# A decoder layer on one core: three of eight token tiles take their experts from streamed blocks in place of gathered rows

## The chip, the cores and the metric

The kernel runs on one core of a Trainium2 chip. The metric is the device time of one execution in microseconds (us), the median of three runs. All arithmetic is fp32. TensorE (PE) multiplies, VectorE (DVE) and ScalarE (ACT) do elementwise work, GpSimd (POOL) issues the gathers, SyncE (SP) issues the direct DMAs. Each engine works off its own instructions in order and waits on semaphores.

## The reference

One layer over 1024 tokens of width 1024: a mixer (attention and pooling, gated and merged), a norm, and then PEER, a mixture of 16384 single-neuron experts, of which each token uses 16 in each of 8 heads, and a last norm:

```python
s = einsum('chpk,hpnk->chpn', q, sub_keys)            # 2 x 128 scores for each head
s1, i1 = top_k(s[:, :, 0], 16);  s2, i2 = top_k(s[:, :, 1], 16)
cand = s1[..., :, None] + s2[..., None, :]            # 256 sums, the best 16 of them
sc, ci = top_k(cand, 16)
idx = row * 128 + col                                 # expert = row * 128 + column
gate = softmax(sc)
act = gelu(einsum('ched,cd->che', u[idx], y))
out = einsum('che,ched->cd', gate * act, v[idx])      # v rows weighted and summed
h = layer_norm(ALPHA * h + out)
```

## The kernel before

Tokens are in 8 tiles of 128 (P). The mixer works on them in three groups of 2, 3 and 3 tiles (`GTS`). All its steps have due times, called ticks here: `unit_at` (products with `w_in`), `step_at` (one step of attention: one head, one tile), `branch_at`, `norm_at`, `query_at`. Each engine has generators that yield such times; `merged` puts them in the order of their times, and `woven` gives a function `advance(tick)` that issues everything that is due by then.

The experts are worked off in slots. A slot t = 128 n + 16 h + e is one gathered row of experts: expert e of head h for each of the 128 tokens of tile n. There are 1024 slots. For each one GpSimd gathers 128 lines of 8 KB (`u` and `v` of an expert side by side, array `uv`) into a ring of 8 (L759). VectorE multiplies the `u` half with the tokens and sums it to one number per token (L1361, `product`). ScalarE takes Gelu for two slots (L950) and multiplies by the gate (L954). Then the `v` half is summed in one of two ways: for even slots, and for all slots from slot 726 on, ScalarE makes a diagonal matrix of the coefficients (L963) and TensorE multiplies it with the row (L1648, `spread`, in two halves, sums kept in PSUM); for 292 odd slots (`by_vector`) VectorE multiplies and adds to `z` (L1313, `add_row`). `join` (L1298, L1300) puts the two sums together, and `norm_step` does the last norm, spread over the slots of the next tile. VectorE also finds the experts, 24 slots ahead, in small steps between the rows: `retrieve`, L1211 to L1276, 64 heads of 18 steps.

The mixer and the slots run together: before slot 0 every engine does the ticks below 0 (group 0), and after each slot t it calls `advance(t)`. So a tick is a slot, and group 1 is due at ticks 0 to about 312, group 2 up to about 726 (its queries and search scores at ticks 598 to 726). Scores of most tiles go to DRAM (`s_scr`) and come back when they are searched; tiles 3 and 4 are parked in `y_scr`.

The lines the change touches in VectorE's loop:

```python
for slot in range(SLOTS):
    product(n, slot)
    if t >= 2 and by_vector(t - 2):
        add_row(t - 2)
    ...                                   # two, one or no steps of the search
    advance(SLOTS * n + slot)
```

Of the kernel before, what the change touches and what calls it, by code (L numbers as in the profile page):

```python
# [8 lines left out]
F32 = mybir.dt.float32  # L9
# [6 lines left out]
P = 128  # L16
# [10 lines left out]
RH = 8  # L27
# [14 lines left out]
DIAGS = 4  # L42
NEG = -3.0e38
PE_AHEAD = 2
# [8 lines left out]
LAST_SLOT = SLOTS * TT  # L53
# [10 lines left out]
DIRECT = T0S[:-1]  # L64
LOADED = [n for n in range(SAVED) if n not in DIRECT]

GATES_AT = (1,) * (H - 1) + (9,)
SEQ = [("p", i) for i in range(NP)] + [(r, 0) for r in "qkv"]
for _h in range(H):
# [10 lines left out]
               tuple(range(598, 598 + 16 * RH + 1, 16)))  # L80
# [10 lines left out]
PARKED = (T0S[1] + 1, T0S[1] + 2)  # L91
# [128 lines left out]
def by_vector(t):  # L220
    if not (24 if t >= SLOTS else 3) <= t % SLOTS < SLOTS - 4:
        return False
    return t % 2 == 1 and t < score_at(NG - 1, RH)

PE_SUMS = list(itertools.accumulate(0 if by_vector(t) else 1 for t in range(LAST_SLOT)))
DVE_SUMS = list(itertools.accumulate(1 if by_vector(t) else 0 for t in range(LAST_SLOT)))

BASED = [n for n in range(TT) if any(by_vector(t) for t in range(SLOTS * n, SLOTS * (n + 1)))]  # L230

# [17 lines left out]
def lent(slot):  # L250

    return slot >= 78 and 14 <= slot % SLOTS < 118

def values_lent(g, k):
    return g > 0 and lent(step_at(g, k) + DO_VALUES[g])

def output_lent(g, k):
    return g > 0 and lent(step_at(g, k) + DO_OT[g])  # L260

def scores_behind(g, k):

    at = step_at(g, k) + DO_OT[g]
    return sum(2 for j in range(NSTEPS[g]) for c in range(len(chunks(g, j))) if score_chunk_at(g, j, c) <= at) + score_no(
        g, 0, 0, 0)

def output_behind(g, k):  # L270

    at = [j for j in range(NSTEPS[g]) if not output_lent(g, j) and step_at(g, j) + DO_OT[g] < step_at(g, k)]
    return STEP0[g] + at[-1] + 1 if g and at else 0

def last_lent(n, is_lent, offset):

    uses = [STEP0[g] + k for g in range(1, NG) for k in range(NSTEPS[g])
            if is_lent(g, k) and (step_at(g, k) + offset[g]) // SLOTS == n]
    return uses[-1] + 1 if uses else 0  # L280

def exponent_at(g):

    begin = TOPK * g - SEARCH_AHEAD + 14
    steps = [step_at(j, k) + DO_EXP[j] for j in range(1, NG) for k in range(NSTEPS[j])]
    return min([slot for slot in steps if begin <= slot < begin + 6], default=begin)

def build(nc, ctx, a, ident, k_scr, v_scr, b_scr, y_scr, s_scr, out):  # L290
# [68 lines left out]
    diag = [at(f"diag{i}", 176 + 0.5 * i, [P, P]) for i in range(DIAGS)]  # L359
# [6 lines left out]
    z = at("z_e", 189, [P, D])  # L366
    yn = at("yn_e", 193, [P, D])
# [63 lines left out]
    def sem(name):  # L431
        return ctx.enter_context(nc.semaphore("r_" + name))
# [1272 lines left out]
```

## Time and profile before

| | |
|---|---|
| median of 3 runs | 3284.1 us (3283.27 to 3287.0) |
| span of the profiled execution | 3285.6 us |
| bytes moved | 1245 MB |
| TensorE, VectorE, ScalarE, GpSimd busy | 2791, 2433, 1145, 1353 us |
| gathers | 1024, of 1.05 MB |

### The profile page before, as it was taken

How to read it: one execution, taken by the hardware profiler on the slowest of the kernel's cores; microseconds unless marked ns; L12 is line 12 of the kernel's file. 1: busy time of each engine (PE TensorE's matmuls, PEld its weight loads, DVE VectorE, ACT ScalarE, POOL GpSimd, SP SyncE). 2: the span in 40 equal slices, each digit the busy share in tenths (PEclk: the TensorE clock that was granted, in tenths of full speed). 3: DMA queues.
4: the chain of work that ended last, by engine and by line, in shares of the span. 5: the costliest groups of instructions: out<-in, count | busy, mean ns of one | idle time of the engine just before them, and what ended most of it. 6: DMA issues, size and time to landing. Idle time of an engine off the chain costs nothing.

```text
span 3285.6 us, 30165 instructions
## 1 busy us (share of the span) xinstructions
PE 2791.3 (85%) x8360; PEld 1440.5 (44%) x8360; DVE 2432.9 (74%) x5863; ACT 1144.9 (35%) x3457; POOL 1353.1 (41%) x1248
## 2 busy tenths in 40 slices
PE   9999999999986899888989898867866777777776
PEld 7776555555433445444444444323433222222222
DVE  2216778995888778997799878798788676667664
ACT  2302455553223333444445322222323333333332
POOL 1101345654434444453455543344445444444442
PEclk9999999999998999999999999989999999999999
DMA  5635999999999999998999999999999999999997
GB/s 195 246 134 200 368 386 371 405 411 369 419 392 411 421 420 404 420 398 332 351 394 385 382 420 420 396 382 421 420 417 420 422 415 417 415 418 416 420 414 311
DMA packets 205223, 1244.97 MB, mean 379 GB/s; under 512 B 23680, under 2 KB 36992, under 8 KB 73600
## 3 DMA queue, kind: packets, MB, share of 16 engines
q0 software_dynamic: 147456, 1073.81, 80.4%
q1 hardware_dynamic: 56592, 169.11, 13.7%
q8 instruction: 67, 1.10, 0.1%
q14 instruction: 100, 0.82, 0.1%
q10 hardware_dynamic: 1008, 0.14, 0.0%
HBM read 1228.81 MB, written 14.16 MB: 378 GB/s over the span
## 4 chain that ended last, share of the span: by engine, by line
PE 44%; DMA 30%; DVE 15%; issue 5%; ACT 4%; POOL 1%; SPq 0%; POOLq 0%; DVEq 0%; ACTq 0%
DMA ring<-uv,idx 29%; PE r_o L1648 16%; PE w_ps L1428 15%; DVE ring L1361 7%; DVE z_e L1313 3%; PE r_o L1614 1%; PE w_ps L1476 1%; PE w_ps L1580 1%; PE w_ps L1557 1%; POOL ring L759 1%; PE w_ps L1614 1%; ACT diag L963 1%; PE r_o L1521 1%; PE r_o L1557 1%; PE r_o L1580 1%
## 5 line engine op out<-in xcount | busy, mean ns | idle before, releaser
L759 POOL DMA_INDIRECT ring<-uv,idx x1024 | 1193.5, 1166 | 1655.6 <-PE r_o L1648 1230.7
L1648 PE MATMUL r_o<-ring,diag 128*128 128x512 f32 x2928 | 1454.8, 631 | 436.6 <-ACT diag L963 424.3
L1361 DVE CUSTOM_DVE_ANT_0 ring<-ring,ytok 128x1024 f32<-128x1024 f32 x768 | 936.7, 1221 | 233.5 <-DMA ring<-uv,idx 230.7
L1648 PEld LDWEIGHTS r_o<-ring,diag 128*128 128x128 f32 x2928 | 542.3, 197 | 1173.7 <-ACT diag L963 643.0
L1428 PE MATMUL w_ps<-x,w 128*128 128x384 f32 (+1 forms) x2112 | 653.0, 456 | 11.0 <-DMA x<-xT 5.7
L950 ACT ACTIVATE gel<-dot 128x2 f32<-128x2 f32 x512 | 104.1, 203 | 1577.1 <-DVE dot L1361 1576.2
L1428 PEld LDWEIGHTS w_ps<-x,w 128*128 128x128 f32 x2112 | 396.9, 192 | 230.6 <-issue 58.7
L1361 DVE CUSTOM_DVE_ANT_0 ring<-ring,zn 128x1024 f32<-128x1024 f32 x256 | 313.3, 1224 | 210.5 <-DMA ring<-uv,idx 209.5
L1313 DVE SCALAR_TENSOR_TENSOR z_e<-ring,coef,z_e 128x1024 f32<-128x1024 f32 x292 | 375.0, 1284 | 0.0
L963 ACT ACTIVATE diag<-ident,coef 128x128 f32<-128x128 f32 x732 | 262.2, 387 | 0.0
L954 ACT ACTIVATE coef<-gel,gate 128x1 f32<-128x1 f32 x1024 | 245.9, 287 | 16.8
L1614 PE MATMUL w_ps<-yT,wq 128*128 128x384 f32 x512 | 190.3, 492 | 0.0
L1614 PEld LDWEIGHTS w_ps<-yT,wq 128*128 128x128 f32 x512 | 100.8, 197 | 103.3 <-issue 70.9
L950 ACT ACT_TABLE_LOAD x94 | 120.6, 1283 | 1.6
L1090 DVE CUSTOM_DVE_ANT_0 e<-w_ps,bias 128x512 f32<-128x512 f32 (+3 forms) x160 | 93.1, 593 | 33.8 <-PE w_ps L1476 32.2
L835 ACT ACTIVATE e<-e,st_a 128x384 f32<-128x384 f32 (+5 forms) x128 | 98.1, 769 | 1.0 <-DVE st_a L1094 0.5
L724 POOL TENSOR_SCALAR st_a<-st_a 128x1 f32<-128x1 f32 x64 | 28.8, 450 | 159.1 <-ACT junk L871 157.5
L1476 PE MATMUL w_ps<-k,q 64*128 64x512 f32 (+3 forms) x320 | 81.2, 585 | 11.9 <-ACT o L861 8.8
L1557 PE MATMUL w_ps<-o,wc 128*128 128x384 f32 x256 | 90.6, 488 | 0.0
L1361 DVE DVE_READ_ACCUMULATOR2_ANT dot<- 128x1 f32 x1024 | 84.7, 83 | 0.0
L848 ACT ACTIVATE aT<-w_ps 128x512 f32<-128x512 f32 (+2 forms) x96 | 46.2, 481 | 85.6 <-PE w_ps L1495 79.9
L1557 PEld LDWEIGHTS w_ps<-o,wc 128*128 128x128 f32 x256 | 48.8, 191 | 42.6 <-issue 19.4
(198 smaller groups left out, 2331.9 us busy)
## 6 DMA issues: line engine op xcount, KB each, us to landing
w<-w_in SPq DMA_DIRECT2D x132, 512.0 KB, 3.7
wq<-wq SPq DMA_DIRECT2D x46, 512.0 KB
wc<-w_branch SPq DMA_DIRECT2D x24, 768.0 KB, 5.7
ring<-uv,idx POOLq DMA_INDIRECT x1024
wo<-w_out SPq DMA_DIRECT2D x24, 512.0 KB, 11.6
xs<-x SPq DMA_DIRECT2D x8, 512.0 KB, 7.5
out<-yn_e SPq DMA_DIRECT2D x8, 512.0 KB
x<-xT SPq DMA_DIRECT2D x16, 192.0 KB, 5.5
```

The lines of the kernel that those rows point to most:

```text
L759: nc.gpsimd.indirect_dma_start(out=ring[t % RING][:], out_offset=None, in_=a["uv"], in_offset=bass.IndirectOffsetOnAxis(ap=idx[:, slot:slo ...
L835: nc.scalar.activation(e[g][k % 2][:, wh, 0:n], e[g][k % 2][:, wh, 0:n], ACT.Exp, bias=nmx[:, wh:wh + 1], accum_out=den[:, wh:wh + 1]).the ...
L950: nc.scalar.activation(gel[:, slot:slot + GROUP], dot[:, slot:slot + GROUP], ACT.Gelu).then_inc(gelu_out, 1)
L954: nc.scalar.activation(coef[:, slot + j:slot + j + 1], gel[:, slot + j:slot + j + 1], ACT.Copy, scale=gate[:, h, e_:e_ + 1]).then_inc(coef ...
L963: nc.scalar.activation(diag[u % DIAGS][:], ident[:], ACT.Copy, scale=coef[:, slot + j:slot + j + 1]).then_inc(diag_ready, 1)
L1313: nc.vector.scalar_tensor_tensor(z[:], ring[t % RING][:, D:], coef[:, slot:slot + 1], z[:], ALU.mult, ALU.add).then_inc(vsummed, 1)
L1361: nc.vector.tensor_tensor_reduce(ring[r][:, 0:D], ring[r][:, 0:D], y_of(n)[:], 1.0, 0.0, ALU.mult, ALU.add, dot[:, slot:slot + 1]).then_in ...
L1428: ins = nc.tensor.matmul(bank, w_raw[g][i % RAWS][:, c, :], x_raw[g][:, c, :], start=c == 0, stop=c == DC - 1)
L1476: nc.tensor.matmul(score_bank(g, wh)[:, 0:n], q[g][h % 2][rows, qs], keys[g][h % 2][rows, begin:begin + n], start=True, stop=True).then_in ...
L1557: ins = nc.tensor.matmul(bank, branch_weights(g, n)[:, j, :], o_all[g][:, j, :], start=j == 0, stop=j == CA - 1)
L1614: ins = nc.tensor.matmul(query_bank(g)[:, 0:WS[g]], query_weights(g, i)[:, c * P:(c + 1) * P], yT[g][c // 4][:, c % 4, :], start=c == 0, s ...
L1648: ins = nc.tensor.matmul(o_ps[n % 2][half][:], diag[(u - 1) % DIAGS][:], ring[t % RING][:, D + half * HALF:D + (half + 1) * HALF], start=s ...
```

## The change

Slots are kept for the first five tiles alone (`GT = 5`, 640 slots). In them VectorE sums every row: `spread`, the diagonals, `join` and the banks lent between the two uses go. Each of two `z` takes every second tile. The sum of a row stands 3 slots behind its product (`LAG`).

The last three tiles (`DT = 3`, 384 tokens) are multiplied with all 16384 experts, in 128 blocks of 128 experts. Block b loads 512 KB of `uT` (3 buffers), TensorE makes the scores of 384 tokens (8 products of 128x384), ScalarE takes Gelu from PSUM, VectorE multiplies by the gates of the block (128x384, most of them zero), and TensorE multiplies with 512 KB of `v` (6 products of 128x512, sums kept in six PSUM banks over all blocks). The scores are 7 blocks ahead of the sums (`LEAD`).

The gates come as follows: the search for the 24 heads of these tiles is the same as before, but its steps follow each other with few rows between (`dense_found`). Rows, columns and shares are transposed; for each of the 384 tokens VectorE makes two one-hot matrices of 128x128 (`dense_hots`), TensorE multiplies them to the 128x128 gates of this token (`places`), ScalarE copies them out, and they go to DRAM (`g_scr`, 12 chunks of 2 MB) and come back for 8 blocks at a time (`gates_in`, 1 KB pieces).

A tick is not a slot any more. `KNOTS` maps slots to ticks: 0 to 165 on 0 to 616, 165 to 187 on 616 to 880, 187 to 640 on 880 to 2092. VectorE, ScalarE, GpSimd and SyncE call `advance(tick_at(t))`. TensorE has no slots left; it does its merged order and waits on semaphores alone. Queries of group 2 take 11 ticks a head in place of 16 and end at tick 686. The dense sums are due from tick 960, 9 ticks a block.

```diff
+GT = 5
+DT = TT - GT
-LAST_SLOT = SLOTS * TT
+LAST_SLOT = SLOTS * GT
...
-               tuple(range(598, 598 + 16 * RH + 1, 16)))
+               tuple(range(598, 598 + 11 * RH + 1, 11)))
...
+NUB, NVB, NGEL, NOH, GQ = 3, 4, 8, 8, 8
+LEAD = NGEL - 1
+EARLY_S = 5
+FOUND_AT = tuple(SCORE_TIMES[2][0] + 18 + 11 * m for m in range(DT * RH + 1))
+TURN_AT = tuple(FOUND_AT[RH * (i + 1)] + 4 for i in range(DT))
+OH_LEN = 3.5
+T_D = TURN_AT[-1] + 6 + int(OH_LEN * P / NOH) + 14
+BLOCK = 9
+KNOTS = ((0, 0), (165, 616), (187, 880), (LAST_SLOT, T_D + BLOCK * NK - 20))
...
+def sum_at(b):
+    return T_D + BLOCK * b
+def dense_at(b):
+    if b < EARLY_S:
+        return SCORE_TIMES[2][RH] + 4 + 5 * b
+    if b < LEAD:
+        return TURN_AT[1] + 2 + 6 * (b - EARLY_S)
+    return sum_at(b - LEAD) + 5
```

SyncE (loads of blocks, gates out and in):

```diff
+        def up_in():
+            for b in range(NK):
+                yield dense_at(b - NUB) + 5 if b >= NUB else norm_at(2, DT) + 12 + b
...
+                sp.dma_start(ub[b % NUB][:], a["uT"][b]).then_inc(u_in[b % NUB], 16)
+        def down_in():
...
+                sp.dma_start(vb[b % NVB][:], a["v"][b * P:(b + 1) * P]).then_inc(v_in[b % NVB], 16)
+        def gates_out():
+            for c in range(CHUNKS):
+                yield hot_at((c + 1) * CHUNK // NOH - 1) + 8
+                sp.wait_ge(place_copied, (c + 1) * CHUNK // 4)
+                sp.dma_start(g_scr[c], stage_g[c % 2][:]).then_inc(g_out[c % 2], 16)
+        def gates_in():
...
+                sp.dma_start(gq[q % 2][:].rearrange("p c r t -> p c (r t)"),
+                             g_scr[:, :, GQ * q:GQ * (q + 1), :].rearrange("c p r t -> p c (r t)")).then_inc(g_in[q % 2], 16)
```

GpSimd, ScalarE and VectorE:

```diff
                 if t >= RING:
-                    if by_vector(t - RING):
-                        pool.wait_ge(vsummed, DVE_SUMS[t - RING])
-                    else:
-                        pool.wait_ge(summed, PE_SUMS[t - RING])
+                    pool.wait_ge(vsummed, t - RING + 1)
...
-                advance(t - RING)
+                advance(tick_at(t - RING + LAG))
...
+                nc.scalar.activation(gel_d[b % NGEL][:], dense_bank(b)[:, 0:DENSE], ACT.Gelu).then_inc(gel_done, 1)
...
-                nc.scalar.activation(diag[u % DIAGS][:], ident[:], ACT.Copy,
-                                     scale=coef[:, slot + j:slot + j + 1]).then_inc(diag_ready, 1)
...
+                for j in range(NOH):
+                    t = NOH * c + j
+                    nc.vector.tensor_scalar(hot_r[u % 2][:, j], count_d[:], turned_d[:, 0, t:t + 1], turned_d[:, 2, t:t + 1],
+                                            ALU.is_equal, ALU.mult)
+                    ins = nc.vector.tensor_scalar(hot_c[u % 2][:, j], count_d[:], turned_d[:, 1, t:t + 1], None, ALU.is_equal)
...
+        def dense_gates():
+            for b in range(NK):
+                yield sum_at(b) - 9
+                dve.wait_ge(gel_done, b + 1)
...
+                nc.vector.tensor_tensor(tokens, tokens, gq[b // GQ % 2][:, :, b % GQ], ALU.mult).then_inc(a_done, 1)
...
-        for n in range(TT):
+        for n in range(GT):
...
                 product(n, slot)
                 t = SLOTS * n + slot
-                if t >= 2 and by_vector(t - 2):
-                    add_row(t - 2)
+                if t >= LAG:
+                    add_row(t - LAG)
...
-                advance(SLOTS * n + slot)
+                advance(tick_at(t))
```

TensorE:

```diff
+        def dense_scores():
+            for b in range(NK):
+                yield dense_at(b)
+                pe.wait_ge(u_in[b % NUB], 16 * (b // NUB + 1))
+                if b >= 2:
+                    pe.wait_ge(gel_done, b - 1)
+                for c in range(DC):
+                    ins = nc.tensor.matmul(dense_bank(b)[:, 0:DENSE], ub[b % NUB][:, c], yT[2][c // 4][:, c % 4, :],
+                                           start=c == 0, stop=c == DC - 1)
+                ins.then_inc(u_done, 1)
+        def dense_sums():
+            for b in range(NK):
+                yield sum_at(b)
+                pe.wait_ge(v_in[b % NVB], 16 * (b // NVB + 1))
...
+                pe.wait_ge(a_done, b + 1)
+                for i in range(DT):
+                    for half in range(2):
+                        ins = nc.tensor.matmul(sum_bank(i, half)[:], gel_d[b % NGEL][:, i * P:(i + 1) * P],
+                                               vb[b % NVB][:, half * HALF:(half + 1) * HALF], start=b == 0, stop=b == NK - 1)
...
-        advance = woven(all_stages(stage))
-        advance(-1)
-        for n in range(TT):
-            for slot in range(SLOTS):
-                if not by_vector(SLOTS * n + slot):
-                    spread(n, slot)
-                advance(SLOTS * n + slot + PE_AHEAD)
+        for _ in merged(all_stages(stage), rcg_turns(), places(), dense_scores(), dense_sums()):
+            pass
```

Smaller parts: all first norms of groups 1 and 2 have their `x` loaded at once, the search scores of all of tiles 0 to 4 but the first four heads go through `s_scr`, the attention of groups 1 and 2 has the banks `o_ps[0]` for its values and outputs, and some semaphores are shared.

## Rows read from the trace of the kernel before

**Rows 1.** The page: span, busy time of each engine, and DMA share in 40 slices.
```profile
span 3285.6 us, 30165 instructions
PE 2791.3 (85%) x8360; PEld 1440.5 (44%) x8360; DVE 2432.9 (74%) x5863; ACT 1144.9 (35%) x3457; POOL 1353.1 (41%) x1248
...
DMA  5635999999999999998999999999999999999997
```

**Rows 2.** Busy time of every engine by stretch; the first line names the columns.
```profile
core 0: us, PE busy (x) PEld busy (x) DVE busy (x) ACT busy (x) POOL busy (x), PEclk, DMA share, GB/s
0.00:302.80 302.80, 289.12 (x1296) 224.81 (x1297) 83.11 (x285) 64.14 (x211) 32.59 (x71) 1.00 0.50 174
302.80:731.00 428.20, 416.42 (x1516) 241.56 (x1515) 367.26 (x919) 216.15 (x585) 213.71 (x190) 1.00 0.98 389
731.00:1300.00 569.00, 501.86 (x1363) 251.32 (x1362) 443.69 (x997) 172.07 (x543) 228.75 (x202) 0.96 1.00 405
1300.00:1900.00 600.00, 530.57 (x1781) 274.68 (x1779) 518.46 (x1246) 272.69 (x731) 297.67 (x266) 0.95 0.97 382
1900.00:2624.00 724.00, 568.84 (x1378) 259.85 (x1379) 580.78 (x1328) 210.89 (x685) 317.65 (x269) 0.94 1.01 413
2624.00:3110.00 486.00, 360.91 (x768) 140.28 (x767) 337.91 (x870) 158.11 (x530) 202.52 (x194) 0.99 1.01 417
```

**Rows 3.** The same for L1361 alone, two records a slot.
```profile
2624.00:3110.00 486.00, 236.47 (x384) 0.99 1.01 417
```

**Rows 4.** The page: DMA queues, with packets, MB and share of 16 engines.
```profile
q0 software_dynamic: 147456, 1073.81, 80.4%
q1 hardware_dynamic: 56592, 169.11, 13.7%
```

**Rows 5.** The page: groups by line; busy us, mean ns | idle before, releaser.
```profile
L759 POOL DMA_INDIRECT ring<-uv,idx x1024 | 1193.5, 1166 | 1655.6 <-PE r_o L1648 1230.7
L1648 PE MATMUL r_o<-ring,diag 128*128 128x512 f32 x2928 | 1454.8, 631 | 436.6 <-ACT diag L963 424.3
...
L1614 PE MATMUL w_ps<-yT,wq 128*128 128x384 f32 x512 | 190.3, 492 | 0.0
...
L950 ACT ACT_TABLE_LOAD x94 | 120.6, 1283 | 1.6
```

**Rows 6.** TensorE: L1614's records (ns min/median/max), two runs of records (start, length).
```profile
L1614 PE MATMUL w_ps<-yT,wq x512: 486/486/847, 1013.7 to 2516.3; 128*128 128x384 f32 x171
...
234.04 27.70 PE r_o L1580 x64
...
2510.36 1.45 PE L1614 MATMUL w_ps<-yT,wq 128*128 128x384 f32 x4
```

**Rows 7.** VectorE in order of time (start, length): a row, and a head's search alone.
```profile
562.48 1.22 DVE L1361 CUSTOM_DVE_ANT_0 ring<-ring,ytok 128x1024 f32<-128x1024 f32 x1
563.62 0.09 DVE L1361 DVE_READ_ACCUMULATOR2_ANT dot<- 128x1 f32 x1
563.62 1.28 DVE L1313 SCALAR_TENSOR_TENSOR z_e<-ring,coef,z_e 128x1024 f32<-128x1024 f32 x1
564.82 0.48 DVE L1224 MAX8 top<-s 128x8 f32<-128x128 f32 x2
...
286.13 0.49 DVE L1211 MAX8 top<-s 128x8 f32<-128x128 f32 x2 [7.46 <-ACT s L912]
...
295.63 0.17 DVE L1274 SCALAR_TENSOR_TENSOR idx<-rc 128x16 uint32<-128x16 f32 x1
```

**Rows 8.** VectorE, single lines: duration ns min/median/max, first and last start.
```profile
L1101 DVE TENSOR_SCALAR st_a<-st_a x64: 272/272/274, 40.8 to 1851.1; 128x1 f32<-128x1 f32 x64
L1083 DVE TENSOR_SCALAR bias<-bias x24: 680/686/690, 26.6 to 1785.2; 128x1024 f32<-128x1024 f32 x24
L1288 DVE TENSOR_SCALAR gate<-gate,esum x64: 222/229/233, 298.8 to 3227.8; 128x16 f32<-128x16 f32 x64
L1047 DVE TENSOR_TENSOR pad<-pad x30: 427/567/620, 11.9 to 1269.7; 128x399 f32<-128x399 f32 x8, 128x397 f32<-128x397 f32 x6, 128x271 f32<-128x271 f32 x4, 128x393 f32<-128x393 f32 x4
```

**Rows 9.** VectorE's waits from 2600 to 3270 us: total, times, longest.
```profile
DVE ring L1361 <- DMA ring<-uv,idx: 216.0, 212, 2.2
```

**Rows 10.** VectorE in order of time: last product and last operation.
```profile
3268.84 1.23 DVE L1361 CUSTOM_DVE_ANT_0 ring<-ring,zn 128x1024 f32<-128x1024 f32 x1 [1.22 <-DMA ring<-uv,idx]
...
3281.29 1.23 DVE L1339 TENSOR_TENSOR yn_e<-yn_e,gb_e 128x1024 f32<-128x1024 f32 x1
```

More of the change, by code:

```diff
@@ L63 @@
 SAVED = KTS[NG - 2]
-DIRECT = T0S[:-1]
-LOADED = [n for n in range(SAVED) if n not in DIRECT]
+HEADS_KEPT = SBUFS
 GATES_AT = (1,) * (H - 1) + (9,)
@@ L217, in final_pad @@
     return 2 - i % 2
[L220 to L230, printed above, removed]
 class Place:
@@ L247, in score_chunk_at, with build @@
     return step_at(g, k) + SCORE_GAP[g] * c
[L250 to L280, printed above, removed]
 def exponent_at(g):
-    begin = TOPK * g - SEARCH_AHEAD + 14
+    begin = tick_at(TOPK * g - SEARCH_AHEAD + 14)
     steps = [step_at(j, k) + DO_EXP[j] for j in range(1, NG) for k in range(NSTEPS[j])]
-    return min([slot for slot in steps if begin <= slot < begin + 6], default=begin)
-def build(nc, ctx, a, ident, k_scr, v_scr, b_scr, y_scr, s_scr, out):
+    return min([tick for tick in steps if begin <= tick < tick_at(TOPK * g - SEARCH_AHEAD + 20)], default=begin)
+def build(nc, ctx, a, ident, k_scr, v_scr, b_scr, y_scr, s_scr, g_scr, out):
     at = Place(nc)
@@ L474, in build, with weights_of @@
     block = ctx.enter_context(nc.Block())
+    def weights_of(r):
+        return len(range(r, UNITS, RAWS))
     def osb_of(g, k):
@@ L647, in scores_out @@
         def scores_out(g):
-            rows = slice(T0S[g] + 1, KTS[g])
+            rows = slice(T0S[g], KTS[g])
             for h in range(RH):
@@ L933, in shares @@
         def shares():
-            for g in range(1, RH * TT):
+            for g in range(1, RH * GT):
                 yield exponent_at(g)
@@ L979, in _ @@
         advance(-1)
-        for n in range(TT):
+        for n in range(GT):
             for slot in range(0, SLOTS, GROUP):
                 coefficients(n, slot)
-                if n and slot == 20:
+                if n and slot == 18:
                     normalize(n - 1)
-                advance(SLOTS * n + slot + GROUP)
-        normalize(TT - 1)
+                advance(tick_at(SLOTS * n + slot + GROUP))
+        normalize(GT - 1)
+        advance(END)
     @block.vector
@@ L1199, in retrieve @@
+        steps_done, steps_d_done = [0], [0]
         def retrieve(g):
             h = g % RH
[L1203 to L1217 removed]
@@ L1269, in retrieve @@
-            assert done == PER * (g + 1)
-            yield
-            dve.wait_ge(step, done)
+            yield from found(scores_of(g), top, topi, topf, s2, cand, cand2, hot, best[:, h], besti, ab, abf, rc[:, 0],
+                             rc[:, 1], step, steps_done)
             if g >= RH:
-                dve.wait_ge(summed, PE_SUMS[TOPK * (g - RH + 1) - 1])
+                dve.wait_ge(vsummed, TOPK * (g - RH + 1))
             nc.vector.scalar_tensor_tensor(idx[:, TOPK * h:TOPK * (h + 1)], rc[:, 0], float(NK), rc[:, 1], ALU.mult,
@@ new lines, in dense_hots @@
+        def dense_hots():
+            per = P // NOH
+            for u in range(DENSE // NOH):
+                i, c = u // per, u % per
+                yield hot_at(u)
+                if c == 0:
+                    dve.wait_ge(rcg_copied, i + 1)
+                if u == 0:
+                    dve.wait_ge(table, 5)
+                    dve.wait_ge(q_unit, HP * NG)
+                if u >= 2:
+                    dve.wait_ge(placed, (u - 1) * NOH // 4)
+                for j in range(NOH):
[3 more added lines that the diff above has]
+                    ins = nc.vector.tensor_scalar(hot_c[u % 2][:, j], count_d[:], turned_d[:, 1, t:t + 1], None, ALU.is_equal)
+                ins.then_inc(hot_ready, 1)
@@ new lines, in dense_scores @@
+        def dense_scores():
+            for b in range(NK):
+                yield dense_at(b)
[6 more added lines that the diff above has]
+                ins.then_inc(u_done, 1)
```

643 lines of the change are left out of this document (405 added, 238 removed).

## The prediction

> **What bounds the kernel now.** I read the page first. The span is 3285.6 us, and TensorE is busy 85% of it, VectorE 74%, the DMA engines 90% and more in nearly every slice after the fifth [rows 1]. Three resources near full over different stretches: so I next read the busy time by stretch [rows 2]. Up to 302.8 us no row is worked on, and TensorE does the mixer of the first group (289 of 303 us). From 302.8 to 731 us TensorE is still full, 416 of 428 us. From 731 us on the DMA engines are (share 0.95 to 1.01, 405 to 417 GB/s). In the last full stretch, 2624 to 3110 us, 192 rows take 486 us, 2.53 us each [rows 2, 3], while VectorE is at 70% and waits 216 us for rows [rows 9]. One row is 128 gathered lines of 8 KB, 1.05 MB. So after about 731 us the kernel costs what its gathers cost, plus the other loads: all 1024 gathers are 1073.8 of 1245 MB [rows 4]. The span stands 1.5 us above the median of the runs, which is nothing here; I sum against the span.
>
> **What the change does to the totals.** It takes away 384 of 1024 gathers (384 x 2.53 = 972 us of DMA). It adds 128 blocks of `uT` and 128 of `v`, 512 KB each. The direct queue moved 169.1 MB in 13.7% of 3285.6 us, 2.66 us per MB [rows 4], so 1.40 us a block, 357 us for all. It adds the gate matrix, 25.2 MB written and 25.2 MB read, 134 us. DMA falls by about 480 us. VectorE loses 384 products and gains 348 row sums, and gets the one-hot rows and the gate products. TensorE loses all 2928 spread records (1454.8 us busy, [rows 5]) and gains the blocks. All three totals end between about 2500 and 2850 us, so in the ideal case the time falls by over 10%. What counts is whether they can be worked off at the same time, and for this I go through the order that `KNOTS` writes down: VectorE, ScalarE and SyncE handle row t only with the mixer's work up to tick_at(t). Rows 0 to 165 go with ticks 0 to 616, rows 165 to 187 with ticks 616 to 880, rows 187 to 640 with ticks 880 to 2092. Before, tick and row were the same, so the same work was spread over 616 rows; now it has to be done by row 165.
>
> **Prices.** Product: the next instruction starts 1.14 us after it (562.48 to 563.62); row sum 1.20 us (563.62 to 564.82) [rows 7]. Search, small parts and norms per row: VectorE is busy 337.9 us for 192 rows in 2624 to 3110 us, 1.76 each, less 1.14, leaves 0.62 with norms, 0.57 without. So a row costs VectorE 2.91 us, against 2.53 us of DMA: with every row summed by VectorE, rows alone are bound by VectorE. A TensorE product in fp32 has two records (256 products of L1614 are x512, [rows 6]); at full clock a record of 512 columns takes 0.433 us (64 in 27.70 us), one of 384 columns 0.32 us (four in 1.45 us, the last 0.49) [rows 6]. A dense block has 8 products of 384 columns and 6 of 512: 16 x 0.32 + 12 x 0.433 = 10.3 us, 1320 us for all.
>
> **Stage A, to the first row.** Unchanged but for which semaphore counts what: 303 us.
>
> **Stage B, rows 0 to 165, ticks 0 to 616.** TensorE: busy 2791.3 less 1454.8 of the spreads less 289.1 of stage A is 1047 us of mixer [rows 1, 2, 5]. The spreads overlap their neighbours (0.59 us long at 0.43 us distance), which hides up to 61 us of the mixer, so 1047 to 1108. The last group's queries are about 95 us of this (half of L1614's 190.3, [rows 5]), and four fifths come after tick 616: 967 to 1028 us are left, I take 1000. VectorE: 165 x 2.91 = 480 us, and the mixer's own 249 us (2432.9 busy, less 83 of stage A, less 1024 x 1.71, less 292 x 1.20): 729. So stage B is TensorE's. It was filled to 97% in 302.8 to 731 us and to 88% in 1300 to 1900 us [rows 2]; now no spread fills the gaps of the attention chain, and a tick is 1.8 us where it was 3, with the same distances in ticks between a product and what uses it. I take 92%: 1087 us; ends 997 (967 at 97%) and 1250 (1028 at 82%). Here VectorE idles some 350 us and the gathers use 417 of 1087 us: what the change saves in traffic is left unused.
>
> **Stage C, ticks 616 to 880, 22 rows.** VectorE does 24 searches of the last three tiles. A head alone, each step waiting for the one before it, takes 9.4 us (286.13 to 295.63, [rows 7]): 226 us. Rows 22 x 2.91 = 64. One-hot rows for two of the three tiles: 768 `tensor_scalar` of 128x128 in all, not in the trace. With two [P, 1] scalars a 128x1 one takes 0.272 us, with an immediate one of 1024 elements 0.686 us, 128x16 with one scalar 0.229 us [rows 8]. Between them and the slope of (0.686 - 0.15) / 1024 per element I take 0.25 and 0.19 us for the two kinds after the usual overlap of 0.085, 0.22 on average; ends 0.13 and 0.34. 768 x 0.22 = 170 us, 114 of it here. With the softmaxes: 410 us (ends 360 and 480). TensorE has under 200 us of work here, the DMA engines 56 us of gathers and the gate matrix's writes. All idle beside VectorE, none of it can be caught up.
>
> **A rule against it.** L759, the gathers' issue, has a mean of 1.17 us on GpSimd and is never the bound here: 41% busy [rows 1, 5]. The Trainium skill (SBUF — State Buffer, "SBUF: two separate sides") says that a VectorE operation in a two-port mode locks GpSimd out of the port pair, so that gathers' descriptors aren't written meanwhile, and fp32 `tensor_scalar` from SBUF is such a one. The trace's L1083 at 0.67 ns per element agrees with the mode, but shows no lock. By the rule the 768 one-hot operations would hold up gathers by at most their 170 us; since 22 rows stand in stage C, which VectorE bounds anyway, it would change the sum by nothing.
>
> **Stage D1, ticks 880 to 960, 30 rows.** 30 x 2.91 = 87, the third tile's one-hots 57, and a wait of the first gate product for the last chunk's way to DRAM and back, taken at 15 (two transfers of 1.5 to 2 MB, 4 and 5.6 us alone, beside gathers; ends 5 and 40): 160 us.
>
> **Stage D2, from tick 960, 423 rows and the 128 blocks.** DMA: 418 gathers not yet under way x 2.53 = 1058 us; some 118 + 124 blocks x 1.40 = 339; 14 gate reads of 1.57 MB, 59; nine tiles of 512 KB in and out, 13; with the remainder some 1480 us. The direct loads also come out at 409 GB/s if mixed with gathers (405 to 413 in [rows 2]), which gives 1450. VectorE: 423 x 2.91 = 1231, 128 gate products of 128x384 at 0.48 us (L1047 has 0.57 for 399, less overlap, [rows 8]) = 61: 1300 us. TensorE: 1320 less seven blocks' first halves, 1284 us. All three are over 85% full, the DMA engines most: 1480 us; ends 1410 and 1640.
>
> **Tail.** Before, 16.7 us from the last product's start to the end [rows 10]. Now the last three row sums, then three tiles' joins, statistics, scale and shift, partly overlapped: 20 us (15 to 35).
>
> Sum: 303 + 1087 + 410 + 160 + 1480 + 20 = 3460 us. That is 5% slower, though DMA, the old bound, has 480 us less to do: it stands idle for some 300 us in C, and in B for 200 to 350 (gathers take 417 of 1087, and all the direct loads of the kernel before were 450).
>
> **Rivals.**
> VectorE is the only bound behind the mixer (faster). It needs the DMA engines to take the dense blocks beside the gathers at no cost, so D2 falls to 1310, and TensorE to be 96% full in B: 303 + 1040 + 410 + 160 + 1310 + 20 = 3243. For it: 97% in [rows 2]. Against it: in every stretch with gathers and loads the share is 0.95 to 1.01 at no more than 417 GB/s. It decides once B and D2 together are under 2390 us. Chance 0.12.
> TensorE becomes the bound in D2 (slower). It is at 87% with bursts and waits in a fixed order. The granted clock was 0.94 to 0.96 in the stretches where TensorE was 79 to 88% busy and 1.00 where it was 97% [rows 2]. At 0.88 with 5% of waits: 1284 / 0.88 x 1.05 = 1530, with worse phases 1650, total 3510 to 3630. The Trainium skill (TensorE: Matmul & The Clock Gate, "HAM oscillation — how this bites in real kernels") has the clock fall in kernels that wait for DMA between bursts; by it the full halving would make D2 2570 us, but then TensorE would have no gaps left, so I don't count this. Chance 0.18.
> The mixer runs in lockstep (slower). In B, ScalarE loads a table of 1.28 us at each change between Exp and Gelu [rows 5], VectorE has a row between any two, and TensorE waits for both: B at 1250 gives 3623. Against it: 95% in stage A, with no rows. Chance 0.13.
> It comes out even: B at 1000 and D2 at 1410 with all else as above gives 3303, with C at 360 3253. Chance 0.05 for this corner.
> The forecast has 0.52. That the change doesn't do what it says isn't likely: the 384 gathers are gone by the loop's bounds.
>
> **From this** slower by over 0.2% (which is about what a measurement of this kernel can tell from no change) has 0.52 + 0.18 + 0.13 and half of the corner, 0.85; within 0.2% 0.02; faster 0.13. The range for 8 in 10 runs from the DMA-cheap corner, 3260, to both slower rivals at their prices, 3640.
>
> **What would show it.** In the trace after: TensorE over 90% busy from 303 to about 1390 us while the DMA share is 0.6 to 0.8 and row 165 comes no earlier; then some 400 us with VectorE full and TensorE under half; then a stretch of about 1500 us with the DMA share near 1 at 3.5 us a row. I am wrong if row 165 is there before 1300 us (TensorE's mixer is shorter than I summed), if a one-hot operation is under 0.13 us, or if the last stretch has a DMA share under 0.9: then VectorE or TensorE sets it.

## The result, and the profile after

| | before | after |
|---|---|---|
| median | 3284.5 us | 3554.6 us (3545.8 to 3558.7, 4 runs) |
| ratio | | 1.0815, 95% interval 1.0800 to 1.0831 |
| span of the profiled execution | 3285.6 us | 3544.0 us |
| bytes moved | 1245 MB | 1035 MB |
| TensorE, VectorE busy | 2791, 2433 us | 2943, 2632 us |

The kernel became 8% slower, though it moves 210 MB less. The page of after, against [rows 1] and [rows 4]:

```profile
span 3544.0 us, 32139 instructions
PE 2943.5 (83%) x9793; PEld 1744.0 (49%) x9793; DVE 2632.1 (74%) x6244; ACT 907.2 (26%) x2305; POOL 882.0 (25%) x866
...
PE   9999999979988889785434498878898998889896
...
DVE  2224556674666668789999789977889888788888
...
PEclk9999999989999999895655599989999999999998
DMA  6635666787655569633336899999999999999996
...
q0 software_dynamic: 92160, 671.13, 48.3%
q1 hardware_dynamic: 122896, 361.54, 27.6%
```

TensorE and VectorE are busy for nearly the same shares of the span as before (83% for 85%, and 74%), but the span is longer. Before, the DMA engines were nearly full in every slice from the fifth on. Now they are in one slice (16) of the first 23 and in slices 24 to 39; slices 18 to 21 have a share of some 0.3. So the page alone shows phases with a different engine full in each, and only one, the last, in which all are near full.

The same by stretch, cut where VectorE's products of rows 0, 165, 187, 217 and 639 begin, against [rows 2]:

```profile
core 0: us, PE busy (x) PEld busy (x) DVE busy (x) ACT busy (x) POOL busy (x), PEclk, DMA share, GB/s
305.10:1441.10 1136.00, 1024.24 (x3801) 607.14 (x3799) 731.18 (x1631) 413.62 (x954) 288.85 (x315) 0.96 0.69 250
1441.10:1853.40 412.30, 244.62 (x967) 181.51 (x966) 370.68 (x1449) 106.01 (x187) 23.72 (x25) 0.74 0.37 135
1853.40:2023.90 170.50, 60.42 (x260) 55.09 (x261) 151.84 (x457) 50.60 (x89) 43.23 (x30) 0.54 0.70 249
2023.90:3507.00 1483.10, 1311.49 (x3448) 669.32 (x3446) 1267.81 (x2384) 266.69 (x857) 490.10 (x421) 0.94 1.00 403
3507.00:3544.00 37.00, 12.28 (x24) 5.04 (x24) 26.88 (x42) 5.64 (x7) 3.23 (x4) 0.73 0.14 57
```

These are stages B, C, D1, D2 and the tail of the prediction. B: TensorE 90% busy, VectorE 64%. C and D1: VectorE 90%, TensorE 52% of 583 us. D2: DMA share 1.00, TensorE 88%, VectorE 85%. Against the sum:

| stage | forecast | measured |
|---|---|---|
| A, to row 0 | 303 | 305.1 |
| B, rows 0 to 165 | 1087 | 1136.0 |
| C, rows 165 to 187 | 410 | 412.3 |
| D1, rows 187 to 217 | 160 | 170.5 |
| D2, rows 217 to 639 | 1480 | 1483.1 |
| tail | 20 | 37.0 |
| sum | 3460 | 3544.0 |

Every stage took longer than forecast, by 84 us in all.

The new groups, from single lines of the trace of after (ns min/median/max), against the prices of [rows 6] and [rows 8]:

```profile
L1446 DVE TENSOR_SCALAR hot_r<-count_d,turned_d x384: 326/345/545, 1575.2 to 1989.0; 128x128 f32<-128x128 f32 x192
L1448 DVE TENSOR_SCALAR hot_c<-count_d,turned_d x384: 273/285/367, 1575.4 to 1989.2; 128x128 f32<-128x128 f32 x192
L1458 DVE TENSOR_TENSOR gel_d<-gel_d,gq x128: 498/550/609, 2017.2 to 3520.1; 128x384 f32<-128x384 f32 x128
L1861 PE MATMUL w_ps<-yT,ub x2048: 486/486/1009, 1547.3 to 3472.8; 128*128 128x384 f32 x187
```

A one-hot operation with two [P, 1] scalars takes 0.345 us, one with one 0.285; in the trace the next starts about 0.09 us before the end, so they cost 0.26 and 0.20 (forecast 0.25 and 0.19). The gate product of 128x384 takes 0.55 us, about 0.47 from start to start (forecast 0.48).

### The profile page after: what moved, and what is told of

Its sections match the earlier page's. It is cut to its first block, busy times and chain, and to the rows that moved or that the text cites. A ratio compares the mean times of both kernels' runs of the same rounds, so it can differ in the third digit from the quotient of the medians.

```text
span 3544.0 us, 32139 instructions
## 1 busy us (share of the span) xinstructions
PE 2943.5 (83%) x9793; PEld 1744.0 (49%) x9793; DVE 2632.1 (74%) x6244; ACT 907.2 (26%) x2305; POOL 882.0 (25%) x866
## 4 chain that ended last, share of the span: by engine, by line
PE 58%; DMA 17%; DVE 16%; ACT 3%; SPq 2%; issue 2%; POOL 0%; DVEq 0%; ACTq 0%
PE w_ps L1634 16%; DMA ub<-uT 13%; PE w_ps L1861 13%; PE r_o L1875 7%; PE w_ps L1808 4%; PE w_ps L1875 3%; DVE z_e L1519 3%; DVE hot_r L1446 3%; PE w_ps L1774 2%; DVE hot_c L1448 2%; PE w_ps L1751 2%; DVE ring L1565 2%; DMA ring<-uv,idx 2%; SPq L719 2%; PE r_o L1719 2%
## 5 line engine op out<-in xcount | busy, mean ns | idle before, releaser
L860 POOL DMA_INDIRECT ring<-uv,idx x640 | 739.5, 1155 | 2342.0 <-DVE z_e L1519 2275.3
L1519 DVE SCALAR_TENSOR_TENSOR z_e<-ring,coef,z_e 128x1024 f32<-128x1024 f32 x640 | 820.9, 1283 | 170.0 <-ACT coef L1092 169.5
L1861 PE MATMUL w_ps<-yT,ub 128*128 128x384 f32 x2048 | 715.0, 505 | 163.6 <-DMA ub<-uT 163.6
L1565 DVE CUSTOM_DVE_ANT_0 ring<-ring,ytok 128x1024 f32<-128x1024 f32 x640 | 781.7, 1221 | 66.5 <-DMA ring<-uv,idx 65.5
L1861 PEld LDWEIGHTS w_ps<-yT,ub 128*128 128x128 f32 x2048 | 403.9, 198 | 481.2 <-DMA ub<-uT 175.2
L1875 PE MATMUL r_o<-vb,gel_d 128*128 128x512 f32 x1024 | 467.0, 599 | 46.0 <-DMA vb<-v 29.6
L1875 PEld LDWEIGHTS r_o<-vb,gel_d 128*128 128x128 f32 x1024 | 196.4, 192 | 270.4 <-issue 209.3
L1850 PE MATMUL r_o<-hot_r,hot_c 128*128 128x128 f32 x768 | 168.9, 409 | 180.1 <-DVE hot_c L1448 180.1
L1850 PEld LDWEIGHTS r_o<-hot_r,hot_c 128*128 128x128 f32 x768 | 156.0, 310 | 194.0 <-DVE hot_c L1448 193.8
L1875 PE MATMUL w_ps<-vb,gel_d 128*128 128x512 f32 x512 | 240.6, 592 | 0.0
L1808 PE MATMUL w_ps<-yT,wq 128*128 128x384 f32 x512 | 184.8, 506 | 20.6 <-DMA wq<-wq 10.5
L1228 DVE RECIPROCAL st_a<-st_a 128x2 f32<-128x2 f32 x64 | 10.5, 164 | 165.0 <-ACT e L937 164.8
```

Of the source, the lines that this page charges most:

```text
L860: nc.gpsimd.indirect_dma_start(out=ring[t % RING][:], out_offset=None, in_=a["uv"], in_offset=bass.IndirectOffsetOnAxis(ap=idx[:, slot:slo ...
L1519: nc.vector.scalar_tensor_tensor(z[n % 2][:], ring[t % RING][:, D:], coef[:, slot:slot + 1], z[n % 2][:], ALU.mult, ALU.add).then_inc(vsum ...
L1565: nc.vector.tensor_tensor_reduce(ring[r][:, 0:D], ring[r][:, 0:D], y_of(n)[:], 1.0, 0.0, ALU.mult, ALU.add, dot[:, slot:slot + 1]).then_in ...
L1808: ins = nc.tensor.matmul(query_bank(g)[:, 0:WS[g]], query_weights(g, i)[:, c * P:(c + 1) * P], yT[g][c // 4][:, c % 4, :], start=c == 0, s ...
L1850: ins = nc.tensor.matmul(place_bank(v)[:, j * NK:(j + 1) * NK], hot_c[u % 2][:, 4 * part + j], hot_r[u % 2][:, 4 * part + j], start=True, ...
L1861: ins = nc.tensor.matmul(dense_bank(b)[:, 0:DENSE], ub[b % NUB][:, c], yT[2][c // 4][:, c % 4, :], start=c == 0, stop=c == DC - 1)
```

## The experiments

Unless a ratio is given, a run is one execution, and the four of the kernel after differ by 13 us among themselves. Stretches that an edit doesn't touch differ by less: B took 1136 to 1144 us and D2 1479 to 1483 us in the runs that leave them alone. Stretches are cut at the same rows as above where `KNOTS` is unchanged; other cuts are named.

**Is the last stretch bound by the DMA engines?** In after, TensorE is 88% busy there, and the rest of its time it waits for `uT`. The waits of 2160 to 3500 us (who for whom: total us, times, longest):

```profile
PEld w_ps L1861 <- DMA ub<-uT: 175.2, 14, 21.6
...
PE w_ps L1861 <- DMA ub<-uT: 163.6, 14, 20.8
DVE z_e L1519 <- ACT coef L1092: 147.9, 28, 17.9
```

The 14 waits of some 12 us are as many as the reads of the gate matrix in this stretch, each 1.57 MB in 1 KB pieces ahead of the `uT` loads in the same queue. So there was a rival: TensorE full but for these waits. Three runs tell it from the forecast's reason.

```diff
-            for q in range(NK // GQ):
+            for q in range(2):
...
-                if b % GQ == 0:
+                if b % GQ == 0 and b < 2 * GQ:
```

> The gate matrix is read back for the first 16 blocks alone; the other 112 blocks are multiplied with the same two buffers, so 14 reads of 1.57 MB are left out and the output is not the layer's. Theory (the last stretch, from row 217 to row 639, is bound by the DMA engines, 1483 us): their traffic falls by 22 MB, 59 us, so the stretch takes about 1425 us and the kernel about 3490. Rival (it is bound by TensorE, which is full but for 163 us in which it waits for uT blocks, once per gate read, because the gate read stands ahead of them in SyncE's queue): with the reads the waits go, the stretch falls to about 1330 us, the kernel to about 3395.

3459.0 us. D2 took 1396.7 us, 86 less:

```profile
2023.30:3420.00 1396.70, 1313.43 (x3448) 661.06 (x3446) 1273.31 (x2385) 266.18 (x857) 451.37 (x421) 0.98 1.01 413
```

That is between the two: more than the bytes' 59 us, less than the waits' 150. TensorE's waits for `uT` are gone from the list of this run, so the reads did cause them. Both have a part: the 1 KB packets took 48 ns each in the trace of after, 64 us for the 14 reads, and some 22 us are left for the waits.

```diff
         def down_in():
-            for b in range(NK):
+            for b in range(NVB):
...
-                pe.wait_ge(v_in[b % NVB], 16 * (b // NVB + 1))
+                if b < NVB:
+                    pe.wait_ge(v_in[b], 16)
```

> Only four of the 128 v blocks are loaded and used again for all others: 124 loads of 512 KB are left out, TensorE's and VectorE's work stays. Theory (DMA engines bound the last stretch): it falls by 124 x 1.40 = 173 us to about 1310, where VectorE (1300) and TensorE (1284) take over; kernel about 3375. Rival (TensorE with its waits behind the gate reads): the waits remain in part, 100 of 163 us, the stretch takes about 1420, the kernel about 3485.

3414.1 us (forecast 3375), D2 1350.0: 133 us less of the 173 that the loads were priced at:

```profile
2025.10:3375.10 1350.00, 1295.29 (x3448) 662.68 (x3446) 1257.70 (x2384) 266.25 (x857) 570.44 (x421) 0.98 0.99 395
```

TensorE is busy 96% and VectorE 93%, so both are near their ends. TensorE's 1295 us agree with the forecast floor of 1284; VectorE's 1258 us are 42 below its 1300. With both so full the stretch ends 40 us above the forecast of 1310; which of the two holds it there, or whether the DMA engines still do (their share is 0.99), no run tells.

```diff
-                for c in range(DC):
+                for c in range(DC // 2):
...
-                                           start=c == 0, stop=c == DC - 1)
+                                           start=c == 0, stop=c == DC // 2 - 1)
```

> Each dense block's scores are made from 4 of its 8 chunks of 128 of the width; all loads stay. TensorE loses 121 x 8 records x 0.32 = 310 us in the last stretch. Theory (DMA engines): the stretch stays at 1480 us, TensorE only waits longer for uT blocks; kernel within 20 us of 3545. Rival (TensorE): the stretch falls to what VectorE needs, 1300 us; kernel 3360.

3519.8 us, 26 below the profiled run of after (forecast within 20), D2 1461.1: 273 us of TensorE's busy time are gone and only 22 us of the stretch. So TensorE isn't the bound of D2. With the 133 us that went with the `v` loads, this leaves the DMA engines.

```profile
2019.50:3480.60 1461.10, 1038.37 (x2480) 493.23 (x2478) 1268.68 (x2384) 266.92 (x857) 498.51 (x421) 0.86 1.01 409
```

**What the gate reads' place in the queue costs.** The same bytes, in quarters:

```diff
-                sp.dma_start(gq[q % 2][:].rearrange("p c r t -> p c (r t)"),
-                             g_scr[:, :, GQ * q:GQ * (q + 1), :].rearrange("c p r t -> p c (r t)")).then_inc(g_in[q % 2], 16)
+                for i in range(4):
+                    if q >= 2 and i:
+                        yield sum_at(GQ * (q - 1)) + 1 + 14 * i
+                    own = slice(3 * i, 3 * i + 3)
+                    sp.dma_start(gq[q % 2][:, own].rearrange("p c r t -> p c (r t)"),
+                                 g_scr[own, :, GQ * q:GQ * (q + 1), :].rearrange("c p r t -> p c (r t)")).then_inc(g_in[q % 2], 16)
...
```

> Each read of the gate matrix (1.57 MB in one DMA ahead of the uT loads in SyncE's queue) is made as four DMAs of a quarter each, 14 ticks apart; all bytes stay. Theory now (the last stretch is the DMA engines', and on top of their time it loses some 25 us because TensorE waits for uT behind a gate read, ScalarE in its order waits for TensorE, and VectorE's row sums wait for ScalarE's coefficients): TensorE's waits for uT fall from 164 to under 60 us, VectorE's waits for coefficients from 148 to under 60 us, and the stretch from 1483 to about 1455 us, no more, since the bytes are the same. Rival (those waits are what sets the stretch): it falls by 85 us or more, to under 1400, as it did when the reads were left out.

3520.1 us, D2 1458.4 (forecast 1455):

```profile
2022.60:3481.00 1458.40, 1333.54 (x3448) 674.64 (x3446) 1269.50 (x2384) 272.33 (x857) 470.63 (x421) 0.95 1.01 410
```

Over the whole of D2 TensorE's waits for `uT` fell from 164 to 105 us (forecast: under 60), in 30 short ones; VectorE's 148 us of waits for coefficients left the list, but its waits for rows rose from 62 to 107 us, and 75 us of waits for the gate reads themselves came. So some 25 us of D2 hung on the place of the reads in the queue. The waits fit this chain: `uT` late behind a gate read, TensorE late, ScalarE waiting in its order for the scores while finished rows waited for their coefficients. The 22 us left over above agree; each is a difference of two single runs, five times what D2 varied without an edit.

**Is the mixer's stretch TensorE's alone?** One line, `KNOTS`, with fewer and with more rows before tick 616:

```diff
-KNOTS = ((0, 0), (165, 616), (187, 880), (LAST_SLOT, T_D + BLOCK * NK - 20))
+KNOTS = ((0, 0), (82, 616), (104, 880), (LAST_SLOT, T_D + BLOCK * NK - 20))
```

> One line is changed: 82 rows in place of 165 go with ticks 0 to 616 (and 22 as before with 616 to 880). Theory (the mixer's stretch is TensorE's alone): it stays at 1136 us though VectorE has 83 x 2.91 = 240 us less to do in it; the 83 rows come in the last stretch at 2.53 us of DMA each, so that it grows from 1483 to 1693 us; kernel about 3755. Rival (lockstep of TensorE, ScalarE and VectorE, with rows in between): the mixer's stretch falls to about 1050 us, the kernel is about 3670.

3710.6 us (forecast 3755, rival 3670). B took 1101.4 us, 35 less. D2, cut at row 136, took 1690.4:

```profile
1981.20:3671.60 1690.40, 1399.14 (x3451) 684.02 (x3452) 1507.90 (x2836) 308.06 (x1000) 585.46 (x504) 0.93 1.01 409
```

It has 81 rows more than in after and took 207 us more, 2.56 us for each. That is the gathers' price of 2.53 and not VectorE's of 2.91.

```diff
-KNOTS = ((0, 0), (165, 616), (187, 880), (LAST_SLOT, T_D + BLOCK * NK - 20))
+KNOTS = ((0, 0), (240, 616), (262, 880), (LAST_SLOT, T_D + BLOCK * NK - 20))
```

> One line is changed: 240 rows in place of 165 go with ticks 0 to 616. Theory: VectorE has 240 x 2.91 + 249 = 947 us in the mixer's stretch, still less than TensorE's 1136, so that stretch grows by less than 40 us; the last stretch has 75 rows fewer, its DMA falls from 1483 to 1293 us, where TensorE (1284, with its gaps 1350) takes over. Kernel about 3440. Rival (the mixer's stretch is in lockstep with VectorE): it grows by the 75 x 2.91 = 218 us and nothing is won, kernel 3600 or more.

3409.3 us (forecast 3440). B took 1202.3 us, 66 more (forecast: less than 40), D2, cut at row 290, 1295.8 (forecast 1350 at most, 1293 of DMA):

```profile
2074.70:3370.50 1295.80, 1273.78 (x3434) 655.13 (x3433) 1052.84 (x1975) 225.92 (x729) 415.10 (x348) 0.99 1.00 402
```

TensorE is busy 98% of it. The mixer's stretches of the two runs, 82 rows first:

```profile
304.30:1405.70 1101.40, 1011.85 (x3784) 602.35 (x3782) 494.59 (x1174) 329.03 (x779) 182.87 (x231) 0.96 0.51 177
```

```profile
304.10:1506.40 1202.30, 1047.69 (x3836) 618.30 (x3835) 941.43 (x2044) 471.03 (x1111) 387.56 (x393) 0.94 0.82 304
```

From 82 to 165 rows a row costs B 0.42 us, from 165 to 240 0.88, against 2.91 us of VectorE's time. So neither theory is right to the end: the stretch is TensorE's, but a row isn't free in it. About a third of the growth is busy time of TensorE (1012, 1024, 1048 us), two thirds are its idle time (90, 112, 155 us). A likely reason, not shown by a run: VectorE, ScalarE and TensorE take turns in the attention chain, and a row between two of its steps makes the step after it late.

**Is the stretch of searches and one-hots VectorE's?**

```diff
-                for j in range(NOH):
+                for j in range(NOH // 4):
```

(and `places` takes `j % 2` for `4 * part + j`)

> VectorE makes a quarter of the one-hot matrices (192 of 768 operations); TensorE multiplies the same two of each eight again, so the gates are wrong and all other work stays. Theory (rows 165 to 217 are bound by VectorE alone): 576 x 0.226 = 130 us are gone, 87 from rows 165 to 187 (412 to 325 us) and 43 from 187 to 217 (170 to 127); kernel about 3415. Rival (TensorE's places, ScalarE's copies of 1.05 us or the chunks' way out and in take their place): under 60 us are gone.

3421.5 us (forecast 3415). C fell from 412.3 to 324.6 us, D1 from 170.5 to 128.3, as forecast to 2 us. Nothing took their place. In after, TensorE waits for these operations; in C alone:

```profile
PE r_o L1850 <- DVE hot_c L1448: 118.9, 31, 6.6
```

**The other half of the change by itself**, on the kernel before:

```diff
-    return t % 2 == 1 and t < score_at(NG - 1, RH)
+    return t < score_at(NG - 1, RH)
```

> The kernel before, with one part of the change alone: the v rows of all slots below 726, but for those at the edges of a tile, are summed by VectorE (the slots are still 1024, nothing is streamed). Theory: a row then costs VectorE 2.91 us against 2.53 of DMA, so slots up to 726 take 726 x 2.91 + 249 = 2362 us behind 303, where they took 2215: kernel about 3410. Rival (VectorE's sums are hidden by the gathers, as VectorE was at 74%): within 15 us of 3284.

3419.5 us (forecast 3410), 137 above its neighbour of 3282.1. Its stretches, cut at the times of [rows 2] but for the first start and the last end:

```profile
306.00:731.00 425.00, 329.01 (x1199) 202.41 (x1198) 408.89 (x902) 185.69 (x496) 205.83 (x177) 0.90 0.96 371
731.00:1300.00 569.00, 395.32 (x1082) 210.54 (x1080) 498.96 (x1047) 149.53 (x468) 235.56 (x202) 0.83 0.98 392
1300.00:1900.00 600.00, 411.18 (x1354) 225.09 (x1355) 564.76 (x1226) 228.63 (x600) 246.40 (x235) 0.81 0.93 352
1900.00:2654.00 754.00, 395.85 (x1069) 210.84 (x1068) 694.16 (x1407) 181.89 (x570) 339.87 (x269) 0.74 0.97 383
```

VectorE is at 96% in the first and 94% in the third, where it was at 86%. TensorE is at 69 to 77% in the first three, where it was at 88 to 97%, and at 53% in the last, where it was at 79%. A row summed by VectorE costs more than its gather. This part of the change loses about 4% before any block is streamed. How much of it is left in the changed kernel, where other work stands around the rows, no run shows.

**A better order of the same work.** With what the runs showed: 120 rows more in B, where one costs about 1 us. Of these, 43 come out of C and D1, where each costs VectorE's 2.91 us, and the others out of D2, where each costs 2.53. The gate reads are in quarters, and the last gate product stands ahead of the fifth tile's norm. The three edits weren't tried apart.

```diff
-KNOTS = ((0, 0), (165, 616), (187, 880), (LAST_SLOT, T_D + BLOCK * NK - 20))
+KNOTS = ((0, 0), (285, 616), (290, 950), (LAST_SLOT, T_D + BLOCK * NK - 20))
...
+        advance(sum_at(NK - 1))
         for slot in range(SLOTS):
             norm_step(GT - 1, slot)
```

> The gate reads in quarters, 285 rows with ticks 0 to 616, only 5 rows with ticks 616 to 950, the rest in the last stretch, and the last gate product ahead of the fifth tile's norm. Theory: the mixer's stretch takes about 1270 us (1202 at 240 rows, then a growing share of VectorE's 2.91 us a row), rows 285 to 290 about 430 us (searches 226, one-hots 174, softmaxes, gates' way), the last stretch 1300 (350 rows: DMA 350 x 2.53 + 411 = 1297, TensorE 1284), the tail 29 in place of 37: 305 + 1270 + 430 + 1300 + 29 = 3334, still slower than the kernel before. Rival (rows in the mixer's stretch cost their full 2.91 us once VectorE is over 85% full there): that stretch takes 1330 us and nothing is won against 240 rows; kernel 3400.

3337.5 us (3333.2 to 3338.7), 1.0146 of the kernel before (interval 1.0123 to 1.0169). Cut at rows 0, 285, 290, 294 and 639:

```profile
303.90:1563.80 1259.90, 1063.35 (x3837) 624.54 (x3836) 1070.41 (x2299) 493.25 (x1189) 452.94 (x440) 0.93 0.87 328
1563.80:1943.30 379.50, 233.35 (x933) 174.71 (x931) 331.98 (x1389) 95.53 (x146) 5.52 (x6) 0.76 0.24 93
1943.30:2029.50 86.20, 35.47 (x259) 32.09 (x259) 68.75 (x274) 34.69 (x41) 3.78 (x3) 0.84 0.45 169
2029.50:3303.60 1274.10, 1273.12 (x3441) 654.67 (x3442) 1039.68 (x1961) 227.10 (x723) 439.67 (x344) 1.00 1.01 406
```

B took 1259.9 (forecast 1270), C and D1 together 465.7 (430), D2 1274.1 (1300), the tail 33 (29). In D2 TensorE is now busy for 1273 of 1274 us at full clock, and the DMA share is 1.01: no order of the same TensorE work within this stretch makes it shorter. What is left are the 466 us of C and D1, in which TensorE does 269 and the DMA engines move a quarter of what they can.

The same with 262 rows by tick 616 and 4 more by tick 950:

> As the run before it, with 262 rows by tick 616 and 4 more by tick 950. Theory: mixer's stretch 1235 us, searches and one-hots 430, last stretch 373 rows, DMA 1355 us, tail 29: 3354 us, 20 above the run with 285 rows. Rival: 20 us or more below it, because 285 rows overfill the mixer's stretch.

3353.1 us (3350.6 to 3359.2), 1.0204 (1.0179 to 1.0228): 16 us above the one with 285 rows (forecast 20), so B isn't overfilled at 285.

## Why the prediction was right

**The direction and the reason.** It said that the DMA engines' 480 us are saved and given back, because the gathers are held to an order in which first TensorE and then VectorE is alone full. The DMA share in B is 0.69 and in C 0.37, where [rows 2] have 0.98 and 1.00; by the shares the DMA engines stand idle for some 350 us in B, 260 in C and 50 in D1. Moving rows by one line, with no work changed, gave 136 us (span 3544.0 against 3407.5), and the best order 217 us of 270 (medians 3554.6, 3337.5 and 3284.5). So most of the loss was in the order, as said. Some 50 us stay; no run traces them to a cause. The size was forecast too small: 5% slower, measured 8%.

**D2.** 1480 forecast, 1483 measured; its bound, the DMA engines, was tested: without 173 us of `v` loads 133 less, with 273 us of TensorE's time gone 22 less. That gathers and loads add up held: 81 rows more in the last stretch made it 207 us longer. But that the sum came within 3 us is in part luck. The packets of D2 in the trace of after, their times added up over the 16 engines, give 1482 us, with misses both ways: 420 gathers took 1069 us (forecast 1058), the 14 gate reads 65 (59), other 1 KB pieces 9 (none), and the blocks and other loads in 4 KB pieces 330 (352), since such a piece took 164 ns, which makes a block 1.31 us and not 1.40. The chain behind the gate reads, some 25 us, wasn't in the sum at all. It doesn't show as idle DMA engines: with the reads in quarters the same packets give 1474 us in a stretch of 1458, so they overlap more. Two readings of the prediction were also off. It says that [rows 2] have 405 to 417 GB/s from 731 us on, but the stretch from 1300 to 1900 us has 382. And the 216 us of [rows 9] are VectorE's waits from 2600 to 3270 us and not from 2624 to 3110. Neither enters the sum.

**C and D1.** 570 forecast, 583 measured. (A head alone is 9.5 us in [rows 7] and not 9.4, 2 us for 24 heads.) The one-hot price, taken between far rows, came out within 0.01 us, and the run with a quarter of them took away 130 us, as summed. The prediction had TensorE under 200 us of work and under half in C; it was busy 245 of 412 us, at a granted clock of 0.74. It wasn't the bound, so this cost nothing. Of the 13 us that are missing, 10.5 are in D1, where VectorE was busy 152 us (sum: 144) and waited 18 us for the first gates (sum: 15).

**B.** The term that was too small, the largest miss: 1000 us of TensorE at 92%. TensorE was busy 1024 us, and its fill was 90%. Of the 49 us missing, 24 are work and 25 are idle time. The work: the mixer's products took 1024 us in B and some 95 behind it, 1119 in all, where the prediction had 1047 to 1108 and went on with a middle value. The granted clock was 0.96 in B, but it was 0.94 to 1.00 in the stretches of [rows 2] that the 1047 us come from, so it doesn't explain the miss by itself. The 61 us by which the spreads hide the mixer have no working in the prediction. The rival of a lockstep had 1250 us; the truth is between: the runs with 82 and 240 rows give a row a price of 0.42 to 0.88 us here, where the forecast had none.

**The tail.** 20 us forecast, 37 measured. This term failed: it counted three tiles' norms partly overlapped, but VectorE alone is busy for 27 of the 37 us, and the fifth tile's norm, which the sum forgot, stands in its order ahead of the last gate product:

```profile
3518.93 1.22 DVE L1545 TENSOR_TENSOR z_e<-z_e,gb_e 128x1024 f32<-128x1024 f32 x1
3520.07 0.55 DVE L1458 TENSOR_TENSOR gel_d<-gel_d,gq 128x384 f32<-128x384 f32 x1
3524.34 1.28 DVE L1468 SCALAR_TENSOR_TENSOR y_d<-y_d,r_o 128x512 f32<-128x512 f32 x2 [3.72 <-PE r_o L1875]
```

TensorE waits 8 us for that gate product with the last block, and the joins of [rows 10]'s kind come three times. Turned round, the tail took 33 us, so the order was worth 4 us of the 17; the rest is the norms' own time.

**The range.** 3260 to 3640 held 3554.6. The median is 10.6 us above the span of the profiled execution, which was the shortest of the four.

**The totals.** The prediction had all three between 2500 and 2850 us; TensorE ended at 2943. This doesn't enter the sum by stages.

**The rivals.** VectorE as the only bound of D2 didn't come: the DMA engines don't take the blocks beside the gathers for nothing. TensorE as the bound of D2 came only when rows were moved out of it. An even result didn't come; the best order found ends 1.5% above.

## What to carry to other kernels

Totals by engine say what a perfect order could reach, not what an order that is written down will reach: take the due times, sum each stage for each engine, and add up the largest of each. Work that frees the bound engine is lost when the freed time falls where that engine can't be used, so look first for the stages in which only one engine is full and move into them what the others could do there. The one-hot price from far rows with the same kind of operand was good to 5%; what the sum lacked most were the price of a row beside the mixer and the full work of the tail.

## What the runs showed of the hardware

**The port pair.** The prediction gave the lock of the two-port mode no weight in the sum, and said that the trace of before shows no lock. The trace of after has three issues that look like one. GpSimd's issues, in order of time (start, length):

```profile
1903.30 1.08 POOL L860 DMA_INDIRECT ring<-uv,idx  x1 [5.21 <-DVE z_e L1519]
1909.59 1.91 POOL L860 DMA_INDIRECT ring<-uv,idx  x1 [5.21 <-DVE z_e L1519]
1912.15 3.47 POOL L860 DMA_INDIRECT ring<-uv,idx  x1 [0.66 <-DVE z_e L1519]
1918.12 3.47 POOL L860 DMA_INDIRECT ring<-uv,idx  x1 [2.49 <-DVE z_e L1519]
```

An issue's median is 0.94 us; the one that begins at 1912.15 lasts until 0.12 us after the end of the 16 one-hots that VectorE makes without a break:

```profile
1911.74 0.40 DVE L1446 TENSOR_SCALAR hot_r<-count_d,turned_d 128x128 f32<-128x128 f32 x1
...
1915.16 0.34 DVE L1448 TENSOR_SCALAR hot_c<-count_d,turned_d 128x128 f32<-128x128 f32 x1
1915.36 1.28 DVE L1565 CUSTOM_DVE_ANT_0 ring<-ring,ytok 128x1024 f32<-128x1024 f32 x1
```

The one-hots beside it also take 0.40 and 0.34 us in place of 0.345 and 0.285, but from start to start they keep 0.26 and 0.20. The Trainium skill (SBUF — State Buffer, "SBUF: two separate sides") states that VectorE in a two-port mode holds GpSimd off for the whole instruction. The three long issues (1912.15, 1918.12 and one at 1924.08 us) agree, except that they last through the rest of a series of 16 such instructions; no issue apart from one-hots took over 2.37 us. The other 16 issues that overlap one-hots don't agree: they took 0.94 to 1.09 us and ended inside the series. They began before it or at most 0.20 us into it, the three long ones 0.41 to 0.43 us into it; whether and why that decides, no run shows. In the trace of before six issues overlap an L1083; they took 1.15 to 1.67 us, but others took up to 2.74 without one, so that trace shows nothing either way. It cost nothing here that can be seen: the one-hots kept their pace, and VectorE was the bound of that stretch, as the run with a quarter of the one-hots showed.

**The DMA share.** It is 0.99 to 1.01 in the last stretch of every variant, at rates from 395 to 413 GB/s, also where TensorE was 96% and VectorE 93% busy and 65 MB fewer were moved. So a share of 1 alone doesn't say that the DMA engines are the bound (with 285 rows in B, TensorE was 100% busy beside a share of 1.01); it took a run with fewer bytes and one with less TensorE work to say which.

**The granted clock.** Its mean over a stretch went roughly with TensorE's busy share: 1.00 where it was 100% busy, 0.94 at 88%, 0.86 at 71% (half the scores), 0.74 to 0.83 at 53 to 69% (all rows summed by VectorE), and 0.54 in D1 at 35%. The busy share alone doesn't fix it: [rows 2] have 0.99 at 74%, and D1 with 285 rows in B had 0.84 at 41%. In C and D1 the lower clock cost nothing that can be seen, as VectorE was 90% and 89% busy. In the kernel before with all rows summed by VectorE, it may be a part of the 137 us; that wasn't tried apart.
